# Position-bias rows of a two-block transformer kernel: from 128 stored copies per head, loaded with a skewed step, to one stored copy per head, loaded with a partition step of one element and read backwards

## The chip, the cores and the metric

The kernel runs on one core of a Trainium2 chip. It is timed as device microseconds (us) of one execution. Its engines are TensorE (PE, the matmuls, with its weight loads as PEld), VectorE (DVE), ScalarE (ACT), GpSimd (POOL) and the DMA queues of SyncE (SP), ACT and POOL, which all use the core's 16 DMA engines.

## What is computed

An activation x of 256 tokens by 2048 features goes through three layers in float32. What matters here is that each has an attention with a bias that depends only on the distance between query and key:

```
# layer 1 (16 heads, top-64 keys of an indexer), layer 2 (32 heads, window 128), layer 3 (8 heads)
h      = rms_norm(x, g) @ w_in
logits = einsum(q, k) * scale + rel_bias[t5_bucket(pos_q - pos_k)]     # bias by distance and head
logits = where(allowed(pos_q, pos_k), logits, -inf)
o      = softmax(logits) @ v
x      = x + (gates * o, other branches) @ w_out
```

Layer 1 has beside it a pooling branch, layer 3 a linear recurrence and a short convolution; a feed-forward part follows. Nearly all of the arithmetic is the product of the activations with the weights, 784 pieces of 512 KB.

## The kernel before, in words

**The weight stream.** The weights are cut into 784 pieces ("subs") of 128 x 1024 float32. SP loads piece after piece into `RAW`, which has four slots (`AHEAD = 4`): the loop in lines 357 to 360 waits on `lo_ready`, that is, until DVE has finished with the piece that was in the slot. ACT copies a piece to `WH` (its float32r part, line 704), DVE subtracts to get the rest `WL` (line 1001), and PE multiplies the piece in three products (`three`, lines 374 to 376), 24 matmuls of 256 columns for a piece. `WH` and `WL` have four slots too, which come free when PE has counted up `subs_used`. So PE works on a piece while ACT and DVE are up to four pieces ahead of it.

**Ticks.** The attention is worked in between pieces: after each piece, each engine calls `tick1(n)` (layer 1), `tick2(n)` or `tick3(n)`, with n the number of the piece in its layer. In layer 1 PE's first four pieces are the keys; ticks 0 to 79 are the ten blocks of projections. At tick 2 PE multiplies one-hot rows by the bias tables (`bias_tables`), and at DVE's tick 3 the results are copied to `ROWS_SB` (lines 1195 and 1196, semaphore `rows_copied`): for each of the three attentions and each head a row of `ROWS = 384` values, bias by distance, with -1e30 where a distance is not allowed. Ticks 17 to 28 are the indexer's scores (`index`, line 524, with `RELU` on ACT), ticks 32 to 47 the top-64 search on DVE (lines 1224 and 1225), tick 34 the sums of squares of the queries (line 548), and the attention of layer 1 begins on PE at tick 50 (line 473).

**The bias.** A tile `B` holds, for four heads, 256 keys for each of 128 queries, one query in a partition. Query p needs a stretch of 256 values of its head's row that begins p values further along than for query 0. The engines need that skew across the partitions, and it is made by way of DRAM: `store_biases` writes each row 128 times to `bias_rows`, one copy for each partition, with a pitch of 385 elements; `load_biases` reads it back with a partition step of 384 elements (`ROWS`), so that each partition starts one element earlier in its copy than the partition before. There are 14 groups of four heads: 14 stores of 768 KB and 14 loads of 512 KB, all from POOL's queue. Each store waits until `subs_used` is at least `10 + 3 * gc`, gc being the number of the group. Nine stores stand before the `affine_select` of the scores, five behind it, and then POOL waits for all of them (`rows_stored`) before it loads the first two groups. The other loads go out where a half of `B` is free (`log_free`).

**Use.** DVE adds `B` to the scaled logits in `attend` (lines 1104 to 1107): the queries of the second half use all 256 keys of `B`, those of the first half its last 128.

Of the kernel before, what the change touches and what calls it, by code (L numbers as in the profile page):

```python
# [33 lines left out]
F32 = mybir.dt.float32  # L34
# [5 lines left out]
P = 128  # L40
T = 256
# [10 lines left out]
DSA_HEADS, SWA_HEADS, MOBA_HEADS = 16, 32, 8  # L52
# [5 lines left out]
ROWS = 384  # L58
# [108 lines left out]
def index_banks(qt):  # L167
# [5 lines left out]
DSA = Attention(DSA_HEADS, HD, 0, [L1_ATTEND + 2 + n for n in (0, 4, 7, 11, 13, 17, 20, 24)])  # L173
SWA = Attention(SWA_HEADS, HD, DSA_HEADS,
                [start + n for start in L2_START for n in ((0, 4, 8, 11) if start < L2_START[3] else (0, 3, 6, 8))])
MOBA = Attention(MOBA_HEADS, MHD, DSA_HEADS + SWA_HEADS, [5, 12, 19, 26])
# [9 lines left out]
def build(nc, x_in, w_in, small_in_dram, tables_in, onehot_in, const_in, out):  # L186
    n_subs = w_in.shape[0]


    bias_rows = nc.dram_tensor("bias_rows", [DSA_HEADS + SWA_HEADS + MOBA_HEADS, P, ROWS + 1], F32,  # L190
                               kind="Internal")
    bias_head = P * (ROWS + 1)
    place = [-(-nc.sbuf_base // 64) * 64]

    def fixed(name, shape, dt=F32):
# [10 lines left out]
    with ExitStack() as ctx:  # L206
# [49 lines left out]
        ROWS_SB = view("ROWS_SB", [32, 3, ROWS], unit(7))  # L256
# [58 lines left out]
        hi_ready, lo_ready, subs_used = sem("hi_ready"), sem("lo_ready"), sem("subs_used")  # L315
# [11 lines left out]
        rows_done, rows_copied, rows_stored = sem("rows_done"), sem("rows_copied"), sem("rows_stored")  # L327
# [662 lines left out]
        def _(dve):  # L990
# [97 lines left out]
            def attend(a, tick, scale, gate=True, mask=None):  # L1088

                u0, bank0, pk0, f0 = BEFORE[a]  # L1090
                L, B = LBUF[a], BBUF[a]
                for u, d, flush in a.due(tick):
                    chunk, qt, _ = a.units[u]
                    bank, fl = bank0 + a.n_banks(u), f0 + a.n_flushes(u)
                    if d == 1:
                        nk, gc = P * (qt + 1), a.row0 // 4 + chunk
                        if qt:
                            dve.wait_ge(bias_in[gc % 2], 16 * (gc // 2 + 1))
                        if u >= 2:
                            dve.wait_ge(pt_ready, pk0 + a.n_packs(u - 1))  # L1100
                        for heads in a.banks(u):
                            dve.wait_ge(log_ready, bank + 1)
                            for m, h in enumerate(heads):
                                ins = dve.scalar_tensor_tensor(
                                    out=L[:, u % 2, h, 0:nk], in0=LOG[:, bank % 2, m * nk:(m + 1) * nk],
                                    scalar=scale(4 * chunk + h, qt), in1=B[:, gc % 2, h, T - nk:T],
                                    op0=ALU.mult, op1=ALU.add)
                            ins.then_inc(log_free, 1)
                            bank += 1
                        dve.wait_ge(log_free, bank)  # L1110
                        if mask is not None:
                            step(dve.tensor_tensor(L[:, u % 2, :, 0:nk], L[:, u % 2, :, 0:nk],
                                                   mask(qt)[:, None, :].to_broadcast([P, 4, nk]), ALU.add))
                        nm = neg_max[:, u % 4, :]
                        ins = dve.tensor_reduce(nm, L[:, u % 2, :, 0:nk], AX_X, ALU.max, negate=True)
                        if a is SWA:

                            step(ins)
                            sink = col("sinks", 4 * chunk, 4)
                            step(dve.scalar_tensor_tensor(out=nm, in0=sink, scalar=-1.0, in1=nm,  # L1120
                                                          op0=ALU.mult, op1=ALU.min))
                            ins = dve.tensor_tensor(sink_d[:, u % 4, :], sink, nm, ALU.add)
                        ins.then_inc(max_ready, 1)
                    t0 = 4 * (a.n_flushes(u) // 2) + (HALF if a is DSA else 0)
                    tf = TF[:, :].rearrange("p (b q) -> p b q", b=4)
                    q = slice(qt * P, (qt + 1) * P)
                    if flush == 0:
                        n = 4 * a.per
                        dve.wait_ge(p_ready, u0 + u + 1)
                        if a is SWA:  # L1130
                            step(dve.tensor_tensor(sums[:, fl % 2, 0:n], sums[:, fl % 2, 0:n],
                                                   sink_e[:, fl % 2, 0:n], ALU.add))
                        step(dve.reciprocal(r_sums[:, 0:n], sums[:, fl % 2, 0:n]))
                        dve.wait_ge(pv_done, pk0 + a.n_packs(u + 1))
                        if fl:
                            dve.wait_ge(ot_ready, fl)
                        dve.tensor_tensor(o_sb[:, :].rearrange("p (h d) -> p h d", h=n),  # L1137
                                          OP[:, :].rearrange("p (h d) -> p h d", h=n),
                                          r_sums[:, 0:n, None].to_broadcast([P, n, a.hd]), ALU.mult)\
                           .then_inc(o_ready, 1)  # L1140
                    if flush == 3:
                        dve.wait_ge(ot_ready, fl + 1)
                        if gate:
                            g = 4 * (a.n_flushes(u) // 2)
                            ins = dve.tensor_tensor(tf, PT[:, :, :], S[:, 16 + g:20 + g, q], ALU.mult)
                        else:
                            ins = dve.tensor_copy(tf, PT[:, :, :])
                        ins.then_inc(ot_taken, 1)
                    if flush == 4:
                        g_lo(GL[:, t0:t0 + 4, q], tf, GH[:, t0:t0 + 4, q])  # L1150
# [93 lines left out]
            for half in range(2):  # L1244
# [3 lines left out]
                for k in range(4):  # L1248
                    t = 4 * half + k
                    ins = dve.scalar_tensor_tensor(out=S[:, 24 + t, :], in0=ps[:, k], scalar=col("pool_scale", t),  # L1250
                                                   in1=S[:, 32 + t, :], op0=ALU.mult, op1=ALU.mult)
# [224 lines left out]
            for t in range(NT):  # L1476
                ins = dve.scalar_tensor_tensor(out=S[:, 16 + t, :], in0=X[:, t, :], scalar=col("g_final", t),
                                               in1=rs[:, :], op0=ALU.mult, op1=ALU.mult)
# [5 lines left out]
        def _(pool):  # L1484
# [21 lines left out]
            def load_biases(a, chunks):  # L1506

                for chunk in chunks:
                    gc = a.row0 // 4 + chunk
                    if chunk >= 2:  # L1510
                        u = a.units.index((chunk - 2, 0, (chunk - 2) % a.per == a.per - 1))
                        pool.wait_ge(log_free, BEFORE[a][1] + a.n_banks(u + 1))
                    elif BEFORE[a][1]:
                        pool.wait_ge(log_free, BEFORE[a][1])
                    src = bass.AP(bias_rows, (a.row0 + 4 * chunk) * bias_head + P - 1,
                                  [[ROWS, P], [bias_head, 4], [1, T]])
                    pool.dma_start(BBUF[a][:, gc % 2], src).then_inc(bias_in[gc % 2], 16)

            step(pool.memset(ones[:, :], 1.0))
# [3 lines left out]
            pool.sem_inc(consts_set, 1)  # L1523
            pool.wait_ge(rows_copied, 1)

            def store_biases(chunks):

                for gc in chunks:
                    pool.wait_ge(subs_used, 10 + 3 * gc)
                    a = MOBA if 4 * gc >= MOBA.row0 else SWA if 4 * gc >= SWA.row0 else DSA  # L1530
                    r = slice(4 * gc - a.row0, 4 * gc - a.row0 + 4)
                    pool.dma_start(bias_rows.ap()[4 * gc:4 * gc + 4, :, 0:ROWS],
                                   ROWS_SB[r, (DSA, SWA, MOBA).index(a), None, :].to_broadcast([4, P, ROWS]))\
                        .then_inc(rows_stored, 16)

            store_biases(range(9))

            pool.wait_ge(score_ready, 1)
            s = SCORE[:, P:].rearrange("p (a k) -> p a k", a=2)
            pool.affine_select(out=s, in_=s, compare_op=ALU.is_ge, fill=FUTURE, base=0,  # L1540
                               pattern=[[0, 2], [-1, P]], channel_multiplier=1).then_inc(score_causal, 1)
            store_biases(range(9, 14))
            pool.wait_ge(rows_stored, 16 * 14)
            load_biases(DSA, (0, 1))

            pool.wait_ge(psum_free, 7)
            width, src = 1, S[:, 24:32, :]
# [34 lines left out]
def shape_constants():  # L1582

    onehot = np.zeros((33, 3, ROWS), np.float32)
    for k, (far, window) in enumerate(((1024, T), (1024, P), (128, T))):
        b = buckets(far)
        for m in range(ROWS):
            n = T - 1 - m
            if 0 <= n < window:
                onehot[b[n], k, m] = 1.0  # L1590
            else:
                onehot[32, k, m] = NEG
    const = np.zeros((P, P + 64), np.float32)
    const[:, 0:P] = np.eye(P)
    for g, w in enumerate(POOL_WINDOWS):
        const[:, P + 16 * g:P + 16 * g + 16] = 1.0 / np.minimum(np.arange(16) + 1, w)
    return onehot, const
# [86 lines left out]
```

## Time and profile before

| | |
|---|---|
| time, three runs | 2601.88, 2598.48, 2600.68 us |
| median | 2600.68 us |
| profiled execution, first to last instruction (span) | 2598.5 us |
| PE busy | 2446.8 us (94%) |
| DVE busy | 1433.4 us (55%) |
| ACT busy | 1064.9 us (41%) |
| POOL busy | 128.6 us (5%) |
| granted TensorE clock, mean | 0.969 |

The profiled execution's own time is known by its span, 2598.5 us, which is also the lowest of the three times. Busy matmul time holds overlaps of pipelined matmuls, so that a busy PE says that it had work and not how fast it went: how many matmuls a stretch holds says that. The granted clock is the share of TensorE's full speed that was granted. Idle time of an engine is put down to what ended it.

### The profile page before, as it was taken

The page shows a single profiled execution, that of the slowest core. Times are in us where ns is not written, and L with a number is a line of the kernel's source. Part 1 is how long each engine was busy: PE and PEld are TensorE (multiplying, and loading weights), DVE is VectorE, ACT ScalarE, POOL GpSimd, SP SyncE. Part 2 cuts the span into 40 slices and gives each one's busy share as a digit, 9 for nine tenths or more (in the row PEclk, how much of TensorE's full clock was granted, in tenths as well). Part 3 has the DMA queues.
Part 4 walks back from the last instruction along what each step waited for, and adds up shares of the span by engine and source line. Part 5 has one row for each costly group of instructions (what it writes and reads, how often), then busy time and mean ns, then how long its engine had stood idle before and what let it go on. Part 6 is the DMA issues. An engine that isn't in the chain of part 4 may idle for free.

```text
span 2598.5 us, 48560 instructions
## 1 busy us (share of the span) xinstructions
PE 2446.8 (94%) x19832; PEld 2419.2 (93%) x19832; DVE 1433.4 (55%) x1666; ACT 1064.9 (41%) x1333; POOL 128.6 (5%) x113
## 2 busy tenths in 40 slices
PE   7676699999988899999999999999999999999997
PEld 7576589999988899999999999999999999999997
DVE  6242466566645564457775455555654554554554
ACT  4121255444545443343654444444443343333342
POOL 0000130110000110000000000001100000000001
PEclk9787799999989999999999999999999999999999
DMA  6767644554433355545555555555555555555553
GB/s 194 131 128 129 153 149 149 185 178 155 148 113 117 126 203 193 176 150 171 171 195 186 181 184 183 174 191 182 172 189 185 185 180 185 182 183 186 180 186 114
DMA packets 126601, 436.51 MB, mean 168 GB/s; under 512 B 20575, under 2 KB 20831, under 8 KB 126440
## 3 DMA queue, kind: packets, MB, share of 16 engines
q1 hardware_dynamic: 113472, 413.19, 48.2%
q0 software_dynamic: 11872, 18.44, 5.1%
q8 instruction: 131, 2.15, 0.3%
q10 hardware_dynamic: 1096, 2.49, 0.3%
q14 instruction: 30, 0.25, 0.0%
HBM read 420.88 MB, written 13.11 MB: 167 GB/s over the span
## 4 chain that ended last, share of the span: by engine, by line
PE 82%; DMA 8%; DVE 5%; ACT 3%; issue 1%; ACTq 0%; SPq 0%; DVEq 0%
PE GP L374 26%; PE GP L376 26%; PE GP L375 26%; DMA RAW<-w_dram 8%; DVE WL L1001 2%; ACT WH L704 1%; PE OP L489 1%; PE PT L455 1%; PE LOG L473 1%; DVE HL L1054 1%; ACT HH L725 0%; PE PT L608 0%; DMA X<-x_dram 0%; PE LOG L548 0%; DVE S L1025 0%
## 5 line engine op out<-in xcount | busy, mean ns | idle before, releaser
L1001 DVE TENSOR_TENSOR WL<-RAW,WH 128x1024 fp32r<-128x1024 f32 x784 | 961.1, 1234 | 1060.6 <-ACT WH L704 1057.5
L704 ACT ACTIVATE WH<-RAW 128x1024 fp32r<-128x1024 f32 x784 | 822.4, 1056 | 1278.9 <-PE GP L376 1060.3
L374 PE MATMUL GP<-HH,WH 128*128 128x256 f32 x4064 | 1178.3, 290 | 59.6 <-DVE WL L1001 59.6
L375 PE MATMUL GP<-HL,WH 128*128 128x256 f32 x4064 | 1166.0, 287 | 0.0
L376 PE MATMUL GP<-HH,WL 128*128 128x256 f32 x4064 | 1165.3, 287 | 0.0
L374 PEld LDWEIGHTS GP<-HH,WH 128*128 128x128 f32 x4064 | 797.3, 196 | 69.9 <-DVE WL L1001 41.5
L375 PEld LDWEIGHTS GP<-HL,WH 128*128 128x128 f32 x4064 | 797.3, 196 | 0.1
L376 PEld LDWEIGHTS GP<-HH,WL 128*128 128x128 f32 x4064 | 796.4, 196 | 0.0
L374 PE MATMUL GP<-GH,WH 128*128 128x256 f32 x2064 | 587.3, 285 | 7.3 <-DVE GL L1062 3.7
L375 PE MATMUL GP<-GL,WH 128*128 128x256 f32 x2064 | 585.8, 284 | 0.0
L376 PE MATMUL GP<-GH,WL 128*128 128x256 f32 x2064 | 585.8, 284 | 0.0
L374 PEld LDWEIGHTS GP<-GH,WH 128*128 128x128 f32 x2064 | 398.0, 193 | 8.1 <-DVE GL L1062 3.9
L376 PEld LDWEIGHTS GP<-GH,WL 128*128 128x128 f32 x2064 | 398.0, 193 | 0.0
L375 PEld LDWEIGHTS GP<-GL,WH 128*128 128x128 f32 x2064 | 398.0, 193 | 0.0
L1500 POOL TENSOR_TENSOR SQACC<-X 128x512 f32<-128x512 f32 x4 | 4.1, 1036 | 1646.2 <-DVE X L1068 1646.2
L1025 DVE TENSOR_TENSOR S<-GP,rs 128x512 f32<-128x512 f32 (+1 forms) x120 | 76.9, 682 | 0.3
L1054 DVE SCALAR_TENSOR_TENSOR HL<-X,small,HH 128x256 fp32r<-128x256 f32 (+1 forms) x64 | 51.2, 858 | 36.1 <-ACT HH L725 36.1
L759 ACT ACTIVATE L<-L,neg_max 128x256 f32<-128x256 f32 (+1 forms) x112 | 49.3, 441 | 0.0
L1062 DVE TENSOR_TENSOR GL<-S,GH 128x1024 f32 (+3 forms) x23 | 29.2, 1271 | 28.5 <-ACT GH L963 20.9
L489 PE MATMUL OP<-V,pts 128*128 128x64 f32 (+1 forms) x336 | 44.1, 275 | 0.4 <-DVE o_sb L1137 0.3
L489 PEld LDWEIGHTS OP<-V,pts 128*128 128x128 f32 x336 | 41.4, 194 | 2.6 <-issue 1.7
L963 ACT ACTIVATE GH<-S 128x1024 f32 (+1 forms) x16 | 17.0, 1060 | 63.6 <-DVE S L1450 63.6
(218 smaller groups left out, 1084.0 us busy)
## 6 DMA issues: line engine op xcount, KB each, us to landing
RAW<-w_dram SPq DMA_DIRECT2D x784, 512.0 KB, 3.7
bias_rows<-ROWS_SB POOLq DMA_DIRECT2D x14, 768.0 KB, 32.2
B<-bias_rows POOLq DMA_DIRECT2D x14, 512.0 KB, 4.5
X<-x_dram ACTq DMA_DIRECT2D x4, 512.0 KB, 10.2
y_dram<-S SPq DMA_DIRECT2D x4, 512.0 KB, 2.6
ONEHOT<-onehot_dram ACTq DMA_DIRECT2D x1, 148.5 KB
small<-small_dram ACTq DMA_DIRECT2D x1, 130.0 KB, 3.9
ident<-const_dram ACTq DMA_DIRECT2D x1, 64.0 KB
```

Source lines behind the costliest of these rows:

```text
L374: pe.matmul(o, wh, rh, start=start, stop=False, skip_group_check=True)
L375: pe.matmul(o, wh, rl, start=False, stop=False, skip_group_check=True)
L376: return pe.matmul(o, wl, rh, start=False, stop=stop, skip_group_check=True)
L455: mm = pe.transpose(PT[:, b, :], ap, ident[:, :])
L473: mm = pe.matmul(LOG[:, bank % 2, m * nk:(m + 1) * nk], q_of(4 * chunk + h, qt), k_of(4 * chunk + h, nk), start=True, stop=True, skip_grou ...
L489: mm = pe.matmul(OP[:, c:c + a.hd], pts[:, (pk + k) % 2, b * P:(b + 1) * P], v_of(4 * chunk + h, kt), start=(c == 0 and kt == 0), stop=(kt ...
L704: act.activation(WH[:, slot], RAW[:, slot], ACT.Copy).then_inc(hi_ready, 1)
L759: ins = act.activation(L[:, u % 2, h, 0:nk], L[:, u % 2, h, 0:nk], ACT.Exp, bias=neg_max[:, u % 4, h:h + 1], accum_out=sums[:, fl % 2, c + ...
L1001: dve.tensor_tensor(WL[:, slot], RAW[:, slot], WH[:, slot].bitcast(F32), ALU.subtract)\
L1025: ins = dve.tensor_tensor(dst(k), ps[:, k:k + 2], rs_of(2), ALU.mult)
L1054: ins = dve.scalar_tensor_tensor(out=HL[:, s, :], in0=X[:, s, :], scalar=small[:, bass.ds(t0 + (SMALL[gain] + k), 1)], in1=HH[:, s, :].bit ...
L1062: dve.tensor_tensor(dst, src, hi.bitcast(F32), ALU.subtract).then_inc(gl_ready, 1)
```

## The change

`bias_rows` in DRAM holds each head's row once (56 rows of 384 values). Three stores, one for each attention, replace the 14 stores, and there is no wait on `subs_used` ahead of them. The loads still fill the same tile with the same 512 KB, but partition p now reads 256 values from element p of the row (partition step 1). To make a step of one element forward do what the skew backward did, the one-hot table is built the other way round, so that the distance grows along a row; in `B` the keys then run backwards, and DVE reads `B` with a step of -1, from element `nk - 1` down to 0. The first two groups are loaded right after the stores, ahead of `affine_select`.

```diff
-    bias_rows = nc.dram_tensor("bias_rows", [DSA_HEADS + SWA_HEADS + MOBA_HEADS, P, ROWS + 1], F32,
-                               kind="Internal")
-    bias_head = P * (ROWS + 1)
+    bias_rows = nc.dram_tensor("bias_rows", [DSA_HEADS + SWA_HEADS + MOBA_HEADS, ROWS], F32, kind="Internal")
...
-                                    scalar=scale(4 * chunk + h, qt), in1=B[:, gc % 2, h, T - nk:T],
+                                    scalar=scale(4 * chunk + h, qt), in1=B[:, gc % 2, h, nk - 1::-1],
...
-                    src = bass.AP(bias_rows, (a.row0 + 4 * chunk) * bias_head + P - 1,
-                                  [[ROWS, P], [bias_head, 4], [1, T]])
+                    src = bass.AP(bias_rows, (a.row0 + 4 * chunk) * ROWS, [[1, P], [ROWS, 4], [1, T]])
...
-            def store_biases(chunks):
-
-                for gc in chunks:
-                    pool.wait_ge(subs_used, 10 + 3 * gc)
-                    a = MOBA if 4 * gc >= MOBA.row0 else SWA if 4 * gc >= SWA.row0 else DSA
-                    r = slice(4 * gc - a.row0, 4 * gc - a.row0 + 4)
-                    pool.dma_start(bias_rows.ap()[4 * gc:4 * gc + 4, :, 0:ROWS],
-                                   ROWS_SB[r, (DSA, SWA, MOBA).index(a), None, :].to_broadcast([4, P, ROWS]))\
-                        .then_inc(rows_stored, 16)
-
-            store_biases(range(9))
-
+            for k, a in enumerate((DSA, SWA, MOBA)):
+                pool.dma_start(bias_rows.ap()[a.row0:a.row0 + a.heads, :], ROWS_SB[0:a.heads, k, :])\
+                    .then_inc(rows_stored, 16)
+
+            pool.wait_ge(rows_stored, 16 * 3)
+            load_biases(DSA, (0, 1))
...
-            store_biases(range(9, 14))
-            pool.wait_ge(rows_stored, 16 * 14)
-            load_biases(DSA, (0, 1))
...
-            n = T - 1 - m
+            n = m - (P - 1)
```

Only POOL's instructions change their order; on PE, DVE, ACT and SP the rows are the same. On POOL, after the constants and ahead of the pooling branch (`WINDOW`), this stood before, with what each instruction waits for in brackets (512x1x384 is the store's four heads by 128 copies, flattened, of 384 values):

```order
L1532 DMA bias_rows<-ROWS_SB 512x1x384 [waits pool_step,subs_used,rows_copied]
L1532 DMA bias_rows<-ROWS_SB 512x1x384 [waits subs_used] x8
L1540 ISA [waits score_ready]
L1540 AFFINE_SELECT SCORE<-SCORE 128x256
L1532 DMA bias_rows<-ROWS_SB 512x1x384 [waits subs_used] x5
L1517 DMA B_109<-bias_rows 128x4x256 [waits rows_stored]
L1517 DMA B_109<-bias_rows 128x4x256
L1551 COPY WINDOW_88<-S 128x8 [waits psum_free]
```

And at the same place of the changed kernel:

```order
L1526 DMA bias_rows<-ROWS_SB 16x384 [waits pool_step,rows_copied]
L1526 DMA bias_rows<-ROWS_SB 32x384
L1526 DMA bias_rows<-ROWS_SB 8x384
L1516 DMA B_109<-bias_rows 128x4x256 [waits rows_stored]
L1516 DMA B_109<-bias_rows 128x4x256
L1533 ISA [waits score_ready]
L1533 AFFINE_SELECT SCORE<-SCORE 128x256
L1541 COPY WINDOW_88<-S 128x8 [waits psum_free]
```

The 14 stores and their waits on `subs_used` are gone, three stores stand in their place, and the first two loads have moved ahead of `affine_select`.

## Rows read from the trace of the kernel before

**Rows 1.** The page: PE's busy time, and the granted clock in 40 slices.

```profile
PE 2446.8 (94%) x19832; PEld 2419.2 (93%) x19832; DVE 1433.4 (55%) x1666; ACT 1064.9 (41%) x1333; POOL 128.6 (5%) x113
...
PEclk9787799999989999999999999999999999999999
```

**Rows 2.** The chain that ended last, 52 to 316 us; pieces are start, us, what.

```profile
by line: DMA RAW<-w_dram 78.6%; DVE WL L1001 6.0%; ACT WH L704 4.0%; PE LOG L548 2.6%; issue 1.3%; PE GP L374 1.2%; PE GP L375 1.0%; PE GP L376 1.0%; ACT SQ L810 0.7%; DVE RK L1036 0.7%; DVE SCORE L1188 0.5%; DVE S L1025 0.5%; PE LOG L473 0
...
63.95 23.79 DMA RAW<-w_dram
...
286.31 23.49 DMA RAW<-w_dram
```

**Rows 3.** Stretches: us, PE, PEld, DVE, ACT, POOL busy (instructions), clock, DMA, GB/s.

```profile
52.00:316.00 264.00, 178.25 (x1178) 169.87 (x1176) 90.78 (x153) 55.81 (x61) 19.51 (x19) 0.80 0.67 131
312.00:480.00 168.00, 158.23 (x1282) 153.92 (x1283) 109.59 (x136) 85.84 (x138) 34.48 (x26) 0.97 0.50 165
1400.00:2000.00 600.00, 599.55 (x4993) 599.24 (x4993) 329.95 (x313) 251.83 (x276) 17.87 (x15) 1.00 0.56 183
```

**Rows 4.** PE in order of time: start, us, line, shape, idle time before it.

```profile
51.68 0.39 PE L374 MATMUL GP<-HH,WH 128*128 128x256 f32 x1
...
315.90 2.09 PE L473 MATMUL LOG<-S 64*128 64x256 f32 x8 [5.10 <-DVEq L1230]
...
318.50 0.41 PE L376 MATMUL GP<-HH,WL 128*128 128x256 f32 x1
318.72 0.41 PE L374 MATMUL GP<-HH,WH 128*128 128x256 f32 x1
```

**Rows 5.** Groups by line, 52 to 316 us: busy, mean ns, idle before, releaser.

```profile
L374 PE MATMUL GP<-HH,WH 128*128 128x256 f32 x360 | 115.3, 320 | 44.3 <-DVE WL L1001 44.3
...
L1001 DVE TENSOR_TENSOR WL<-RAW,WH 128x1024 fp32r<-128x1024 f32 x45 | 58.3, 1295 | 171.2 <-ACT WH L704 170.3
L704 ACT ACTIVATE WH<-RAW 128x1024 fp32r<-128x1024 f32 x46 | 48.6, 1056 | 204.6 <-DMA RAW<-w_dram 188.6 <-PE GP L376 15.7
...
L524 PE MATMUL LOG<-S 64*128 64x256 f32 (+1 forms) x64 | 14.6, 362 | 18.9 <-ACT RELU L807 16.4 <-DVE S L1025 2.4
...
L548 PE MATMUL LOG<-pair,SQ 128*128 128x2 f32 x32 | 7.0, 353 | 17.5 <-ACT SQ L810 17.5
```

**Rows 6.** DMA queues and issues, 52 to 312 us: packets, MB, share; us to landing.

```profile
q0 software_dynamic: 9856, 11.10, 41.9%
q1 hardware_dynamic: 6120, 22.28, 25.2%
...
RAW<-w_dram SPq DMA_DIRECT2D x42, 512.0 KB, 22.0
bias_rows<-ROWS_SB POOLq DMA_DIRECT2D x14, 768.0 KB, 32.2
```

**Rows 7.** The same view, 312 to 480 us.

```profile
q1 hardware_dynamic: 6688, 24.35, 43.6%
...
RAW<-w_dram SPq DMA_DIRECT2D x47, 512.0 KB, 3.7
B<-bias_rows POOLq DMA_DIRECT2D x6, 512.0 KB, 4.9
```

**Rows 8.** PE groups by form, 480 to 840 us.

```profile
L473 PE MATMUL LOG<-K,S 64*128 64x256 f32 x64 | 10.3, 402 | 1.8 <-DVE L L1104 1.8
L608 PE MATMUL PT<-pair,SQ 128*128 128x2 f32 x64 | 8.0, 255 | 3.1 <-ACT pts L768 1.9 <-ACT SQ L851 1.2
L473 PE MATMUL LOG<-K,S 64*128 64x128 f32 x64 | 5.8, 297 | 0.0
```

**Rows 9.** Line 1517, the 14 loads of B: POOL's idle time and landing.

```profile
  DVE L L1104: 321.3, 9
  DMA bias_rows<-ROWS_SB: 36.5, 1
...
DMA to landing us min/median/max: 4.1/4.5/6.9
```

**Rows 10.** DVE's additions of B, 312 to 480 us.

```profile
L1104 DVE SCALAR_TENSOR_TENSOR L<-LOG,rq,B 128x256 f32<-128x256 f32 (+1 forms) x32 | 11.1, 409 | 0.9 <-ACT S L815 0.9
```

## The prediction

> **What bounds the kernel now.** I read the page first: PE is busy for 94% of the span, and the granted clock is full in most slices but falls in the second to the fifth, about 65 to 325 us [rows 1]. So the kernel is bound by PE with one disturbed stretch near its start. To see what a healthy stretch looks like I took 1400 to 2000 us: 4993 matmuls in 600 us, one every 0.120 us, with PE never idle [rows 3]. A piece of weights is 24 matmuls, 2.88 us. Between 52 and 316 us there are only 1178 matmuls in 264 us [rows 3]. The chain of waits says why: 78.6% of this stretch is waiting for `RAW<-w_dram`, in nine parts of 20 to 26 us, the first at 63.95 and the last at 286.31 us [rows 2]. ACT stands idle 188.6 us for these transfers, DVE then 170.3 us for ACT, PE 44.3 us for DVE [rows 5].
>
> The DMA view tells what makes them late. A weight transfer lands 22.0 us after its issue here and 3.7 us after it between 312 and 480 us [rows 6, 7]. Its own work is no larger: 25.2% of 16 engines over 260 us is 1048 engine-us for 42.5 transfers of 512 KB (22.28 MB), 24.7 each; later 43.6% over 168 us is 1172 for 46.4, 25.2 each. The rest is POOL's queue. Its 41.9% is 1743 engine-us, and the 14 stores take 32.2 us each, 451 us together, so a store holds 1743 / 451 = 3.9 engines as long as it lasts [rows 6]. A weight transfer is complete only when its slowest engine is, so it waits in each of its parts for the four engines that carry a store. The stretch begins where the stores begin and ends where the last has landed: POOL waits 36.5 us for that [rows 9], then loads the first `B`.
>
> The Trainium skill (DMA: Bandwidth & Descriptors, Rules for kernel authors) says that the slowest dimension sets how many engines a DMA uses; a store with four heads outermost would then be confined to four, and the new ones, with 16, 32 and 8 rows outermost, would use 16, 16 and 8. The trace's 3.9 agrees.
>
> **The change part by part.** *The 14 stores go (11 MB), three of 24, 48 and 12 KB come.* All the loss of the stretch should go with them. From the start of tick 6's piece at 51.68 us to PE's first attention matmul at 315.90 us [rows 4] PE does 3 x 360 = 1080 weight matmuls [rows 5], which is 45 pieces; at 0.120 us they are 129.6 us. Beside them stand the indexer's 64 records at line 524 (half with 256 columns, half with 128) and 32 records at line 548 [rows 5]. Undisturbed, between 480 and 840 us, the same forms take 10.3 / 64 = 0.16, 5.8 / 64 = 0.09 and 8.0 / 64 = 0.125 us [rows 8]: 32 x 0.16 + 32 x 0.09 + 32 x 0.125 = 12.0 us. PE's work is 141.6 us where it now takes 264.2: 122.6 us lost. They show twice in the trace: PE idle 44.3 + 18.9 + 17.5 + 5.1 = 85.8 us [rows 4, 5], and the rest, 36.8 us, is PE at a granted clock of 0.80 on the mean [rows 3], which after each idle time falls to the lower level (1.2 GHz): one matmul then takes 0.22 us [rows 4]. The slow clock goes on behind the stretch: the eight records at 315.90 take 2.09 us instead of 8 x 0.16 = 1.28, and from 318 to about 321 us 14 matmuls take 0.215 instead of 0.120. That is 0.8 + 1.3 = 2.1 us more. It is tempting to take the chain's 78.6% of 264 us, 207 us, as the price; PE works beneath those waits, so I count PE's matmuls instead.
>
> *What could hold the stretch instead.* For one piece ACT takes 1.06 us and DVE 1.23 to 1.3; in all DVE is busy 90.8 us for the 45 pieces with indexer and top-64 search, 2.0 us a piece, and ACT 55.8, 1.2 [rows 3, 5]. Both are under PE's 3.15 (141.6 / 45), and both run up to four pieces ahead. The waits at lines 524 and 548 on ACT, and the 5.1 us for DVE, are of engines made late by the weights. Still, the next stretch (312 to 480 us, with no store) leaves PE idle 9.8 of 168 us, 5.1 of them the wait just named [rows 3, 4], so 4.7 are of its own. In proportion I take 4 us for small waits in mine.
>
> *The stores' place.* Issued at once after `rows_copied`, each with a few dozen rows, they should land in the time of a load, 4 to 7 us [rows 9], and POOL has nothing else to do then. `affine_select` is now behind the two loads and not behind nine stores: no later, since it waits for tick 30 of DVE. The pooling branch waits on `psum_free` as before.
>
> *The loads.* They are as many and as large, 14 of 512 KB in runs of 1 KB, and land in 4.1 to 6.9 us [rows 9]. What is new is that 128 partitions read nearly the same 1.5 KB of each head's row. The trace has no such read. Bounds: no loss (now 4.5 us), or that of the store, which reads one row in SBUF 128 times and needs 32.2 us for 768 KB [rows 6]. I take the first, since the fetch is from DRAM with all 16 engines, and keep the second as a rival. What a late weight transfer costs: SP issues piece k+4 when DVE is through with k, 2.3 us after PE finished k-4; ACT wants it 4 x 2.88 = 11.5 us after that point, 9.2 us later, and PE then has three pieces in store less 2.3 us of splitting, 6.3 us. So one transfer may land in up to 15.5 us before PE feels it. A load that lands in 10 us is hidden.
>
> The Trainium skill (same page, Latency and other measured facts) speaks against such reads: per-partition streams that run in lock step at a pitch of 4 MiB or more got half the rate, 103 instead of 207 GB/s, and it infers that they meet in one HBM channel. Rows this near to each other might meet likewise; with half the rate a load would land in about 10 us, under the cushion, and the sum would stay the same. No row here shows it.
>
> *The reversed read.* 112 additions (eight for each of 14 groups), 11.1 us for 32 or 0.35 each by that sum, 0.41 on the mean of one [rows 10]. Float32 with one operand in PSUM; I take no change. If a step of -1 doubled them, 11.1 us would be added where DVE is busy 109.6 of 168 us [rows 3]: mostly hidden, at most 112 x 0.41 = 46 us if none were.
>
> **Sum.** 2598.5 (this profiled execution) - 122.6 - 2.1 + 4 = 2477.8. The median of the runs is 2.2 us above that execution: 2480.
>
> **Rivals.**
> *A. Other waits hold the stretch.* With late weights gone, the ring of PE, ACT and DVE through the indexer and the search might not keep up. For it: lines 524 and 548 show waits of 7 to 17 us. Against it: the busy sums. At the pace of the stretch from 312 to 480 us (47 pieces in 168 us, 3.57 each [rows 7]) the 45 pieces take 161 us: gain 103 + 2, time 2496.
>
> *B. Slower loads or a slower reversed read.* If loads land in 18 to 20 us they cost 3 to 4 us each beyond the cushion, 50 us in all; a doubled addition costs 5 to 20 us where it stands ahead of PE. Time 2490 to 2530.
>
> *C. The other side: the loads become the new stores.* If all partitions' reads of one small region went at the pace of the stores or worse, 16 engines would be held and weights come late again, 14 times, spread over the run. The stall is the landing less 15.5 us. It eats the gain of 125 us from 125 / 14 = 8.9 us a load, a landing of 24.4 us, 5.4 times today's 4.5. At the store's 32.2 us the price is 14 x 16.7 = 234 us less 125: 2710. For it: only the store's row. Against it: the store was on four engines, these are on sixteen, and four engines' pace on sixteen is 32.2 / 4 x 512 / 768, about 5.4 us.
>
> *D. The stores are not what delays the weights.* Then nothing changes, 2601. Against it: onset and end agree with the stores to a few us, and the engine time is accounted for.
>
> **How the numbers follow.** Forecast 69%, A 12%, B 12%, C 5%, D 2%. Own range of the forecast 2473 to 2488: no small waits at all, or three times those I took. The range must leave out no more than two in ten: it takes in A and most of B, 2471 to 2525, which leaves C, D and the worst of B outside. About 0.2% of the time, 5 us, is what a measurement of this kernel can tell from no change. Faster is forecast, A and B: 0.94, with D the same at 0.02, slower C at 0.04 (a mild C still gains).
>
> **What the changed profile would show.** Step 1: weights landing at about 3.7 us between 52 and 197 us, and no `RAW<-w_dram` to speak of in the chain. Step 2: PE's first attention matmul at about 197 us instead of 315.90, some 1180 matmuls before it, clock near 1.00. Step 3: stores landing under 7 us, `B` loads at 4 to 7; 10 to 15 would be the half rate, still free. Step 4: line 1104 at 0.41 us. Step 5: everything from the attention of layer 1 on takes as long as before, 2598.5 - 315.9 = 2282.6 us, less 2. I am wrong if `B` lands in over 15 us with weight waits beside it, if PE waits for ACT or DVE in the indexer, or if a late stretch grows.

## The result and the profile after

The changed kernel takes 2482.57 us (median of 4 runs, 2479.18 to 2483.42), the kernel before 2599.63 us in the same session (4 runs). The ratio is 0.9545, 95% interval 0.9532 to 0.9559: 117 us faster. The forecast was 2480, in the range 2471 to 2525.

The page of the changed kernel, its busy times and the granted clock, and the chain that ended last (shares of the span by engine):

```profile
PE 2416.2 (97%) x19832; PEld 2392.3 (96%) x19832; DVE 1435.8 (58%) x1666; ACT 1066.1 (43%) x1333; POOL 113.5 (5%) x102
...
PEclk9999999998999999999999999999999999999999
...
PE 92%; DVE 5%; ACT 2%; issue 1%; DMA 0%; ACTq 0%; DVEq 0%
```

The dip of the clock in the second to fifth slice [rows 1] is gone, and so is the DMA from the chain. PE in order of time: the start of tick 6's piece, and the first matmuls of layer 1's attention:

```profile
51.72 0.39 PE L374 MATMUL GP<-HH,WH 128*128 128x256 f32 x1
...
203.16 1.14 PE L473 MATMUL LOG<-S 64*128 64x256 f32 x8
```

The work that took from 51.68 to 315.90 us [rows 4] now takes 151.4 us. The stretch and the one behind it (columns as in [rows 3]):

```profile
52.00:203.00 151.00, 151.00 (x1176) 145.81 (x1175) 92.06 (x153) 55.92 (x60) 6.34 (x5) 0.98 0.50 164
203.00:360.00 157.00, 151.12 (x1235) 147.13 (x1235) 104.34 (x126) 81.61 (x134) 27.99 (x23) 0.98 0.47 155
```

PE does as many matmuls (1176 against 1178) and is never idle. The groups of this stretch, to set beside [rows 5]:

```profile
L374 PE MATMUL GP<-HH,WH 128*128 128x256 f32 x360 | 104.6, 291 | 0.0
...
L704 ACT ACTIVATE WH<-RAW 128x1024 fp32r<-128x1024 f32 x45 | 47.7, 1060 | 92.3 <-PE GP L376 92.2
...
L524 PE MATMUL LOG<-S 64*128 64x256 f32 (+1 forms) x64 | 13.6, 343 | 0.0
...
L548 PE MATMUL LOG<-pair,SQ 128*128 128x2 f32 x32 | 4.0, 260 | 0.0
```

ACT now waits for PE to free a slot (92.2 us) where it waited 188.6 us for DMA. The DMA view of 52 to 203 us, and from the views of the two lines on POOL, the landing of the three stores and of the 14 loads:

```profile
q1 hardware_dynamic: 6442, 23.51, 47.0%
q0 software_dynamic: 288, 1.05, 2.3%
...
RAW<-w_dram SPq DMA_DIRECT2D x44, 512.0 KB, 3.4
...
DMA to landing us min/median/max: 1.7/1.8/2.2
...
DMA to landing us min/median/max: 3.8/4.9/7.0
```

A weight transfer lands in 3.4 us instead of 22.0 [rows 6]. The loads of `B`, whose 128 partitions now read nearly the same row, land as they did (4.1/4.5/6.9 [rows 9]). The reversed additions on DVE, 203 to 371 us:

```profile
L1104 DVE SCALAR_TENSOR_TENSOR L<-LOG,rq,B 128x256 f32<-128x256 f32 (+1 forms) x32 | 11.1, 409 | 1.2 <-ACT S L815 1.2
```

11.1 us for 32, 409 ns on the mean, to the digit what it was [rows 10]: a step of -1 costs nothing here.

### The profile page after: what moved, and what is told of

The parts are those of the page before. It is cut to its first block, busy times and chain, and to the rows that moved or that the text cites. A ratio compares the mean times of both kernels' runs of the same rounds, so it can differ in the third digit from the quotient of the medians.

```text
span 2481.5 us, 48548 instructions
## 1 busy us (share of the span) xinstructions
PE 2416.2 (97%) x19832; PEld 2392.3 (96%) x19832; DVE 1435.8 (58%) x1666; ACT 1066.1 (43%) x1333; POOL 113.5 (5%) x102
## 4 chain that ended last, share of the span: by engine, by line
PE 92%; DVE 5%; ACT 2%; issue 1%; DMA 0%; ACTq 0%; DVEq 0%
PE GP L374 29%; PE GP L375 29%; PE GP L376 29%; DVE WL L1001 1%; PE OP L489 1%; PE PT L455 1%; PE LOG L473 1%; ACT WH L704 1%; DVE HL L1054 1%; PE LOG L524 1%; ACT HH L725 0%; PE PT L608 0%; DMA X<-x_dram 0%; DVE X L1068 0%; DVE S L1477 0%
## 5 line engine op out<-in xcount | busy, mean ns | idle before, releaser
L374 PE MATMUL GP<-HH,WH 128*128 128x256 f32 x4064 | 1166.6, 287 | 15.1 <-DVE WL L1001 15.1
L374 PEld LDWEIGHTS GP<-HH,WH 128*128 128x128 f32 x4064 | 786.9, 194 | 22.7 <-issue 20.4
L375 PEld LDWEIGHTS GP<-HL,WH 128*128 128x128 f32 x4064 | 786.8, 194 | 0.1
L376 PEld LDWEIGHTS GP<-HH,WL 128*128 128x128 f32 x4064 | 786.1, 193 | 0.0
```

The costliest lines, as they stand in the source:

```text
L374: pe.matmul(o, wh, rh, start=start, stop=False, skip_group_check=True)
L375: pe.matmul(o, wh, rl, start=False, stop=False, skip_group_check=True)
L376: return pe.matmul(o, wl, rh, start=False, stop=stop, skip_group_check=True)
```

## The experiments

The kernels' lines shift by a few, so that 704 may read 707.

**The old stores kept beside the new loads.** This takes the load and the reversed read alone. Of the edit only the added stores are shown; `store_biases` and its waits stay, and the loads, the reversed read and the one-hot table are those of the change.

```diff
+    bias_once = nc.dram_tensor("bias_once", [DSA_HEADS + SWA_HEADS + MOBA_HEADS, ROWS], F32, kind="Internal")
...
+            for k, a in enumerate((DSA, SWA, MOBA)):
+                pool.dma_start(bias_once.ap()[a.row0:a.row0 + a.heads, :], ROWS_SB[0:a.heads, k, :])\
+                    .then_inc(rows_stored, 16)
             store_biases(range(9))
```

> The changed kernel's compact rows, its loads with a partition step of one element and its reversed read, but the 14 stores of 768 KB stay where they stood, into a tensor that nothing reads, and POOL waits for them before it loads the first two groups. Theory Q (the 14 stores alone make the weights late): 2600 us, weights landing in about 22 us between 52 and 312 us, and with the twelve later loads undisturbed the rest as in the changed kernel. Rival L (the new loads or the earlier start of the first two also took part in the gain): clearly under 2600, say 2560 or less. If the new loads or the reversed read cost something that the gain has covered, this comes out above 2602.

Measured: 2599.55 us, ratio to the kernel before 0.9996 (0.9986 to 1.0005). Weights land in 22.6 us between 52 and 312 us. The gain belongs to the stores, and the new loads and the reversed read neither cost nor bring anything beyond the interval, some 4 us. Rival L's other half, the earlier start of the first two loads, is not in this kernel. The trace of the kernel before shows that it had nothing to give: nothing waits there for a load of line 1517, and DVE's first addition of `B` stands at 324.8 us, 12.9 us after the first of these loads was issued. Of the prediction's rivals D falls here; A, B and C fell with the result (PE never idle, 151.4 us and not 161, loads of `B` landing in 3.8 to 7.0 us).

**The same bytes by 16 heads at a time.**

```diff
-                    pool.dma_start(bias_rows.ap()[4 * gc:4 * gc + 4, :, 0:ROWS],
-                                   ROWS_SB[r, (DSA, SWA, MOBA).index(a), None, :].to_broadcast([4, P, ROWS]))\
+                    pool.dma_start(bias_rows.ap()[4 * gc:4 * gc + n, :, 0:ROWS],
+                                   ROWS_SB[r, (DSA, SWA, MOBA).index(a), None, :].to_broadcast([n, P, ROWS]))\
...
-            store_biases(range(9))
+            store_biases((0, 4, 8))
```

> The kernel before, with the same bytes stored by four DMAs instead of 14: 16, 16, 16 and 8 heads outermost instead of four, at the same counts of pieces (10, 22, 34, 46). Theory Q4 (what hurts is that each store holds four engines while a weight transfer waits for its slowest part; the same packets on 16 engines take fewer microseconds in all): a store of 16 heads has on each engine as many packets as a store of four heads had on its four, so 4 x 37 = 148 us of disturbed stream instead of 260; some 22 pieces pass in it instead of 51, less the cushion: loss about 75 us, time about 2557. Rival B (the bytes and packets count, however they lie on the engines): as before, 2600. Rival W (16 slow packets at a time are worse, since every part of every weight transfer waits): above 2600.

Measured: 2527.58 us, ratio 0.9725 (0.9707 to 0.9743): 45 us over the changed kernel where 75 were expected. Its DMA view, 52 to 240 us:

```profile
q0 software_dynamic: 2816, 11.01, 50.7%
...
RAW<-w_dram SPq DMA_DIRECT2D x42, 512.0 KB, 7.0
bias_rows<-ROWS_SB POOLq DMA_DIRECT2D x3, 3072.0 KB, 34.9
bias_rows<-ROWS_SB POOLq DMA_DIRECT2D x1, 1536.0 KB, 34.4
```

3072 KB on sixteen engines land in 34.9 us, 768 KB on four in 32.2 [rows 6]: an engine's pace is nearly the same. The engine time is of the same order too (50.7% of 16 x 188 us is 1525 engine-us, against 1743), but the stores last 139 us here, three times 34.9 and once 34.4, and not 260. So it is not the bytes that count, but how long any engine is held. This confirms the direction of theory Q4. Its size was too large: the four stores cost 45 / 4 = 11 us each, not 19. The 7.0 us is a median over weight transfers issued during the stores and between them; those issued between 56 and 91 us, mostly during the first store, land in 22.2 us, as late as before, but there are four such times instead of 14.

**The pitch in DRAM.**

```diff
-    bias_rows = nc.dram_tensor("bias_rows", [DSA_HEADS + SWA_HEADS + MOBA_HEADS, P, ROWS + 1], F32,
+    bias_rows = nc.dram_tensor("bias_rows", [DSA_HEADS + SWA_HEADS + MOBA_HEADS, P, ROWS], F32,
...
-                                  [[ROWS, P], [bias_head, 4], [1, T]])
+                                  [[ROWS - 1, P], [bias_head, 4], [1, T]])
```

> The kernel before with one number changed: the copies in DRAM stand at a pitch of 384 elements instead of 385, so that each run of 1536 B starts at a multiple of 512 B, and the loads step by 383 elements. Same 14 stores, same engines, same source. If the slow packets of the stores come from where the runs start in DRAM, a store lands in about 8 us and the time is near the changed kernel's, 2485 to 2500. If they come from the source (one row of one partition read 128 times) or from the four engines, the stores land in about 32 us as before and the time is 2600.

Measured: 2598.36 us, ratio 0.9998 (0.9988 to 1.0007), stores landing in 32.4 us. So whether the runs start at a multiple of 512 B in DRAM does not matter.

**Lone stores.** Added to the changed kernel in the feed-forward part, from `DUMMY`, a tile of zeros in four partitions:

```diff
+            for gc in range(14):
+                pool.wait_ge(psum_free, MIX_BLOCK + 24 + 4 + 1 + 2 * gc)
+                pool.dma_start(copies.ap()[4 * gc:4 * gc + 4, :, 0:ROWS],
+                               DUMMY[:, None, :].to_broadcast([4, P, ROWS])).then_inc(rows_stored, 16)
+            pool.wait_ge(rows_stored, 16 * 17)
```

> The changed kernel with 14 of the old stores added in the feed-forward part, one every 16 pieces of weights (46 us), from zeros, into a tensor that nothing reads: each store stands alone. A weight transfer may land up to 15.5 us after its issue before PE feels it. By the packets: while a store lasts some 37 us its four engines pass one weight packet for each store packet, 5.4 pieces instead of 12.8; 7.4 pieces late are 21 us, less the cushion of about 12: 9 to 10 us a store, 14 x 9.5 = 133 us, time about 2615. Rival H (a store that stands alone is hidden by the four slots, only crowded stores hurt): 2483. Both agree that the stretch from 52 to 200 us is as in the changed kernel.

Measured: 2695.8 us, ratio 1.0361 (1.034 to 1.0382): 213 us over the changed kernel, 15.2 a store, not 9.5. The store issued at 1999.87 us, in stretches of 4 us (columns as in [rows 3]):

```profile
2012.00:2016.00 4.00, 4.00 (x35) 4.00 (x35) 0.00 (x0) 0.00 (x0) 0.00 (x0) 1.00 0.52 123
2016.00:2020.00 4.00, 2.57 (x22) 2.37 (x20) 0.00 (x0) 0.00 (x0) 0.00 (x0) 1.00 0.59 131
2020.00:2024.00 4.00, 0.00 (x0) 0.00 (x0) 0.00 (x0) 0.00 (x0) 0.00 (x0) 0.59 0.26 47
2024.00:2028.00 4.00, 0.00 (x0) 0.00 (x0) 1.22 (x1) 1.06 (x1) 0.00 (x0) 0.50 0.26 43
2028.00:2032.00 4.00, 3.94 (x22) 3.94 (x23) 0.01 (x1) 0.00 (x0) 0.00 (x0) 0.63 0.58 139
2032.00:2036.00 4.00, 1.63 (x9) 1.43 (x9) 1.23 (x1) 1.81 (x2) 0.00 (x0) 0.79 0.31 87
```

ACT and DVE have run dry by 2012, PE works on the pieces it has in store until about 2019 and is idle until 2028, and comes back at the lower clock (22 matmuls in 4 us instead of 35). Rival H is refuted: four slots do not hide one store. My size was off in two ways. I let one weight packet pass for each store packet, 5.4 pieces in a store's time; between 2008 and 2036 us ACT could start on three, at 2025.69, 2032.45 and 2035.25 us, where 5.4 in 37 us would have been four. And I left out the slow clock behind the wait.

**Extra stores from all partitions, and from four partitions but other addresses.** `DUMMY` has 128 partitions here. The source of the extra stores changes, and in the first of the two kernels the order of the 512 rows with it:

```diff
-                pool.dma_start(copies.ap()[4 * gc:4 * gc + 4, :, 0:ROWS],
-                               DUMMY[:, None, :].to_broadcast([4, P, ROWS])).then_inc(rows_stored, 16)
+                pool.dma_start(copies.ap()[4 * gc:4 * gc + 4, :, 0:ROWS].rearrange("h p r -> p h r"),
+                               DUMMY[:, 0:4, :]).then_inc(rows_stored, 16)
```

> The kernel of the lone stores (14 extra stores of 768 KB in the feed-forward part, into a tensor that nothing reads), but each store now takes its 512 rows of 1536 B from 128 partitions, four rows from each, instead of one row of each of four partitions 128 times; the place in DRAM and the runs written are the same. Theory S (the stores are slow because of where they read: few engines, each on one partition): they land in 4 to 8 us and cost nothing under the cushion, time about 2484. Rival R (runs of 1536 B into DRAM are slow from anywhere): on 16 engines with 11 packets of 0.7 us each they land in about 9 us, and cost 0 to 2 us each, 2484 to 2510; packet time tells, from the landing.

```diff
-                               DUMMY[:, None, :].to_broadcast([4, P, ROWS])).then_inc(rows_stored, 16)
+                               bass.AP(DUMMY, 0, [[32 * ROWS, 4], [92, P], [1, ROWS]])).then_inc(rows_stored, 16)
```

> The same extra stores, 512 rows of 1536 B from four partitions as before, but each row from its own place (steps of 368 B along the partition) and not the same 1536 B again and again. If the pace is set by reading one address over and over, they now land in well under 36 us (four engines at the pace of a load: about 10 us) and the time falls from 2696 towards 2500. If it is set by one partition for each engine, or by the runs written, landing stays at 34 to 37 us and the time at about 2696.

Measured: 2480.92 us from all partitions, ratio 0.9542 (0.9528 to 0.9557), nothing lost against the changed kernel's 0.9545; and 2706.88 us from four, ratio 1.0409 (1.0393 to 1.0425). The DMA views from 1750 us on, first of the stores from all partitions (710 us long), then of those from four (890 us):

```profile
q0 software_dynamic: 2688, 11.01, 4.4%
...
copies<-DUMMY POOLq DMA_DIRECT2D x14, 768.0 KB, 5.5
```

```profile
q0 software_dynamic: 9856, 11.10, 12.2%
...
copies<-DUMMY POOLq DMA_DIRECT2D x14, 768.0 KB, 37.0
```

The same 11 MB in the same runs of 1536 B to the same places take 4.4% x 16 x 710 = 500 engine-us from 128 partitions and 12.2% x 16 x 890 = 1737 from four. So two things made a store last 32 us: four engines instead of 16, and 3.5 times the time on an engine. Both went away together when the rows came from 128 partitions. Reading other addresses in four partitions does not help (by the medians it came out 11 us slower than the lone stores), and neither do sixteen engines with one partition each: the stores of 16 heads made 2816 packets of the same bytes in 1525 engine-us, 0.54 us a packet, where 128 partitions make 2688 packets in 500, 0.19 us a packet. So the number of packets does not set the pace either. What the slow stores moved comes to about 6 GB/s for each partition that they read: 768 KB from four in 32.2 us are 24 GB/s, 3072 KB from sixteen in 34.9 us 90 GB/s. Two readings of this are left, and no run separates them: that one partition serves an engine only so fast, or that neighbours hinder each other, since the slow stores all read partitions that lie side by side (four, eight or sixteen in a row). A store from four partitions far apart would tell. The store from all partitions also reads four rows that lie one behind the other in a partition, and writes the rows to DRAM in another order; that this plays no part is not shown either.

**The indexer's matmuls of two ticks together.** On the changed kernel:

```diff
-                if n - L1_INDEX - 1 in range(12):
+                if n - L1_INDEX - 1 in range(0, 12, 2):
                     index(n - L1_INDEX - 1)
+                    index(n - L1_INDEX)
```

> The changed kernel, with the indexer's score matmuls of two ticks issued together at every second tick, so that the heads in the lower half of PE's rows are followed by those in the upper half, as the attention's logits are. My price for these matmuls was taken from the attention's; they took 12 x 1.06 us instead of 8.0, and each tick 0.2 us of change-over. Theory: the pair then takes 1.07 us like the attention's eight, six pairs 6.4 to 7 us and six change-overs, 7 us saved: 2475 to 2477. Rival (the price is that of the operation, wherever it stands): pairs of 2.1 us, only six change-overs saved, 2481 to 2482.

Measured: 2476.86 us, ratio 0.9524 (0.9511 to 0.9537), at the upper end of what was expected, 5.7 us under the changed kernel. Pieces of the chain (start, us, records), first of the changed kernel, then of this one:

```profile
86.54 1.06 PE LOG L524 x4
90.67 1.06 PE LOG L524 x4
...
119.55 1.08 PE LOG L524 x8
```

```profile
86.52 1.07 PE LOG L524 x8
93.54 1.07 PE LOG L524 x8
...
114.60 1.64 PE LOG L524 x16
```

With 256 columns, eight records of both halves of PE's rows take as long as four of one half; with 128 columns, sixteen take 1.64 us where eight take 1.08. The two ticks of a pair also write to the two PSUM banks of `LOG` in turn, so that the half and the bank are not told apart here. In the changed kernel a piece with its tick takes 90.67 - 86.54 = 4.13 us: 24 x 0.12 = 2.88, 1.06, and 0.19 of change-over.

**The narrow matmuls in two halves.** On the kernel of the last experiment; the loop over `qt` gives way to one half for each of the two ticks:

```diff
-                if n == L1_QUERIES + 2:
+                if n in (L1_QUERIES + 2, L1_QUERIES + 3):
+                    qt = n - L1_QUERIES - 2
```

> The kernel of the paired indexer ticks, and the 32 narrow records at line 548, after which the granted clock fell for 6 us with PE never idle, are done in two halves, 16 after tick 34 and 16 after tick 35. If 1.9 us of two-column matmuls at a time leave the clock up, 2.6 us more are saved: 2473 to 2475. If the clock falls after each half, it costs up to 2.6 us more than the kernel without the split: 2476 to 2480.

Measured: 2472.93 us, ratio 0.9512 (0.9499 to 0.9525), just under what was expected and the fastest kernel here. The same 25 us, first of the kernel with the paired ticks alone, then of this one:

```profile
140.00:165.00 25.00, 25.00 (x187) 25.00 (x187) 13.83 (x33) 7.97 (x8) 0.00 (x0) 0.86 0.40 129
...
140.00:165.00 25.00, 25.00 (x213) 25.00 (x213) 15.99 (x37) 9.29 (x9) 0.00 (x0) 1.00 0.47 162
```

PE does 26 matmuls more in the second, at 0.12 us some 3.1 us of work. Stretches of 5 us, of the changed kernel and then of this one:

```profile
150.00:155.00 5.00, 5.00 (x40) 5.00 (x40) 2.79 (x8) 1.06 (x1) 0.00 (x0) 0.85 0.47 144
155.00:160.00 5.00, 5.00 (x26) 5.00 (x25) 0.00 (x0) 0.17 (x1) 0.00 (x0) 0.50 0.17 66
160.00:165.00 5.00, 5.00 (x42) 5.00 (x42) 2.87 (x5) 1.95 (x2) 0.00 (x0) 0.97 0.28 98
```

```profile
150.00:155.00 5.00, 5.00 (x43) 5.00 (x44) 2.05 (x4) 1.30 (x2) 0.00 (x0) 1.00 0.34 108
155.00:160.00 5.00, 5.00 (x44) 5.00 (x43) 4.42 (x13) 1.69 (x3) 0.00 (x0) 1.00 0.30 105
```

In the changed kernel the 32 records at line 548 take 3.8 us, and the clock is at its lower level for 6 us behind them though PE is never idle. In halves of 1.68 us, with a piece of weights between them, it stays up. The intervals of this kernel and of the one before it overlap, so that their difference, 3.9 us by the medians, is seen better in the clock than in the time.

## Why the prediction was right, step by step

**What bounds the stretch.** Right. The stores made the weights late, and with the stores kept nothing is gained. The rule of the Trainium skill (DMA: Bandwidth & Descriptors, Rules for kernel authors) that the outermost dimension sets the number of engines agrees with the 3.9 engines of [rows 6]. It is only part of the cause, though: with sixteen engines a store lasted as long, 34.9 us, for four times the bytes. And that each weight transfer waits for the engines under a store is argued, from the landing of 22 us beside stores; no trace here tells the engines apart.

**The price.** I counted PE's matmuls and not the chain's 207 us of waiting; the stretch became 112.8 us shorter (264.2 to 151.4), not 207. Term by term, the stretch was to take 129.6 + 12.0 + 4 = 145.6 us and took 151.4:
- the indexer's matmuls, 8.0 us in the sum, took 12 x 1.07 = 12.8. I had taken their price from the attention's [rows 8], where heads of both halves of PE's rows (and with them both banks) follow each other; the same form with the same columns is dearer where they don't. The two-tick experiment showed it. The change-overs between them and the weight matmuls, 12 x 0.19 = 2.3 us, were not in the sum at all;
- the clock behind the narrow matmuls was not in it: some 28 matmuls at 0.21 instead of 0.12, 2.6 us. The halves showed it;
- the 4 us for small waits were not there: PE is busy for all of the 151 us.

129.6 + 12.8 + 2.3 + 4.0 + 2.6 = 151.3. The errors, +7.1 and +2.6 against -4, leave the stretch 5.8 us longer than forecast. The 9.7 us are also what was wrong with my reading of the loss: of the 122.6 us that I called lost, 36.8 of them to the slow clock, 9.8 did not come back: dearer matmuls, change-overs and a dip of the clock that the changed kernel has too.

The rest of the run, from the first attention matmul on, takes 2481.5 - 203.2 = 2278.3 us, where I had 2280.5. That these 2.2 us offset part of the 5.8 is luck; they are within the spread of the runs (2479.18 to 2483.42). So the path and the mechanism were right, and that the time came within 3 us of 2480 is in part luck: the small waits were put in as a guard and stood in for terms that I had not seen. The lower end of the forecast's own range, 2473, does not follow either: with no small waits at all the sum gives 2476.

**The span and the time.** I took the profiled execution of before for the lowest of the three runs, since its span has the same number, and added 2.2 us. In the runs that list both, the time is 1.9 us above the span (2483.42 and 2481.5 for the changed kernel). The term is nearly right for another reason.

**The loads and the read.** Right, both at nothing. The half rate that I weighed as a possibility did not show: loads of `B` landed in 3.8 to 7.0 us, where it would have been about 10.

**The cushion.** It was not needed for the result. As a number it did not hold: lone stores cost 15.2 us, not 9.5. The threshold of 15.5 us for one late transfer, and so the landing of 24.4 us from which rival C would decide, are not confirmed by any run.

**What stays open.** An engine is some 3.5 times slower when the stores read four or sixteen neighbouring partitions than when they read all 128. Whether that is one partition for each engine, the neighbourhood or the order of the rows was not taken apart; nor how an engine divides its turns between the two queues.

## What to carry to other kernels

Before you skew or copy data by way of DRAM, ask which partitions the transfer reads and how long it holds any one engine: a stream that needs all 16 engines is as late as the slowest of them, so that in the feed-forward part 11 MB from four partitions cost 213 us, and 11 MB from 128 partitions nothing. Here the 11 MB from four cost 117 us. A load can make the skew itself, by a partition step of one element, from a row that is stored once. To price the removal of a stall, count the bound engine's work at its undisturbed pace in the same order of operations; the waits of the chain overstate it, here 207 for 113 us.

## What was not expected of the hardware

- By their medians, 768 KB from four partitions landed in 31 to 37 us, 3072 KB from sixteen in 34.9 us, 768 KB from 128 partitions in 5.5 us.
- Matmuls over 64 rows are cheaper when the lower and the upper half of PE's rows, each with its own bank, follow each other: 8 records in 1.07 us where 4 of one half take 1.06.
- After 3.8 us of two-column matmuls the clock was at its lower level for 6 us with PE busy throughout; after 1.68 us of them, twice with a piece of weights between, it stayed at the upper one.
- A step of -1 on a float32 operand of DVE's additions cost nothing (409 ns both ways), and neither did 128 partitions reading one small region of DRAM (loads in 3.8 to 7.0 us against 4.1 to 6.9).
